# Products of zeros on TensorE ahead of ten steps of a two-block hybrid network

## The chip, the cores and the metric

One core of one Trainium2 chip runs the whole program in one launch. The metric is the device time of one execution in microseconds (us), as the median of several runs. TensorE is called PE in the profile, its weight loads PEld, VectorE DVE, ScalarE ACT, GpSimd POOL, and the queue that issues the DMAs SP.

## What is computed

256 tokens of width 1024 pass through two blocks of two layers each, all in float32.

```
# block 1, for each of 2 layers
h = x @ w_in                                  # q, k, v of three attentions, index, forget gate, gate
a  = subln(diff_attention(...)); b = sparse_attention(top 64); c = forgetting_attention(...)
mixed = concat(a, b, c) * silu(gate)
x = layer_norm(ALPHA * x + mixed @ w_out)
# block 2, for each of 2 layers; xs = 256 latent tokens, cs = 256 context tokens
hx = rms_norm(xs) * (1 + scale) + shift       # scale, shift, gate come from silu(c) @ w_mod
px = hx @ w_in + b_in
ya = conv_module(...)                         # depthwise convolution of 31 taps
yb = (rms_norm(gla_forward + gla_backward) * silu(gate)) @ w_gla_out     # gated linear attention
yc = (grouped_attention(...) * silu(gate)) @ w_attn_out
xs = xs + gate_x * ((sigmoid * ya + sigmoid * yb + sigmoid * yc) @ w_out)
```

## The kernel before

**How a product is made.** A float32 product is split. Each operand is written as hi + lo, both rounded to a float32 form that PE multiplies in one pass; three products (hi·hi, lo·hi, hi·lo) replace one. A weight piece of 128 x 1024 arrives by DMA (L3115), ACT makes its hi part (`cut_hi`, L1920) and DVE its lo part (`cut_lo`, L2340). Four cut pieces fit in block 1, three in block 2, so the cut of a piece waits until PE has finished with the one that had its place. Activations are turned by PE against the identity (`flip`, L1468), ACT takes the hi part from the bank (`flip_hi`, L1954), DVE the lo part (`flip_lo`, L2349). `project` is six products of 512 columns (L1541 to L1543; in block 2 a bias product, L1537, goes ahead), `project_t` the same for transposed outputs (L1559 to L1561).

**Order.** A planner writes one list of steps; each engine runs its own steps of that list strictly in order and waits on semaphores. An output bank of PE is taken in turn from a pool, and a step waits for the reader of its bank's last content (`before`).

**Places that the change touches.** `out1` is block 1's output projection: half 0 takes the mix in the order of parts 1, 0, 0, 2 (`MIX_PAIRS`), for two token tiles. The mix part 0 of a tile is ready late, at the end of the differential attention. After `out1` come the residual (L2563), the layer norm on DVE and POOL, and the flips of the new x (`flip x1`) for the next layer. `flip y1` turns the gated output of linear attention, which POOL makes (`gated`, L2995), after the token tiles' head norms, in POOL's order. `mod` are the products of block 2's modulation (L1482), put between block 1's steps. `in2` with chunk 3 (`KKV`) is the first projection of block 2's latent tokens.

The head of `project` before the change, which decides what PE waits for:

```python
        xh, xl = operand(kind, l, kp, t)
        pe.wait_ge("cut_lo", n)
        if kp == 0:
            pe.wait_ge(*(before or ()))
```

Of the kernel before, what the change touches and what calls it, by code (L numbers as in the profile page):

```python
# [8 lines left out]
F32, F32R, BF16 = mybir.dt.float32, mybir.dt.float32r, mybir.dt.bfloat16  # L9
# [3 lines left out]
P = 128  # L13
# [12 lines left out]
WC = 512  # L26
# [46 lines left out]
VAL, GLU, CGATE, KKV, GV, LRQ, AQ, GG, AG, M0A, M0B, M1A, M1B, M2A, M2B = range(len(CHUNKS2))  # L73
# [45 lines left out]
def tiles_of(layer):  # L119
    return EVERY if layer < LAYERS - 1 else X_TILES  # L120
# [22 lines left out]
def pipeline(items, stages, lags):  # L143
    for tick in range(len(items) + lags[-1]):
        for stage, lag in reversed(list(zip(stages, lags))):
            if 0 <= tick - lag < len(items):
                yield from stage(items[tick - lag])


def flip(source, l, t, g):  # L150
# [75 lines left out]
def attend(l, name):  # L226
    for qt in range(NT):
        key = lambda j: (l, name, qt, j)
        scores = lambda j: iter([[("att_s",) + key(j)]])
        top = lambda j: iter([[("att_max",) + key(j), ("att_exp",) + key(j), ("att_norm",) + key(j)]])  # L230
        turn = lambda j: iter([[("att_flip",) + key(j), ("att_t_act" if j % 2 == 0 else "att_t_dve",) + key(j)]])
        values = lambda j: iter([[("att_v",) + key(j)]])
        yield from pipeline(range(MAPS[name]), [scores, top, turn, values], [0, 1, 3, 4])
        yield [("att_out_diff", l, qt) if name == "diff" else ("att_out", l, name, qt)]
# [971 lines left out]
class Program:  # L1206
# [19 lines left out]
    def allocate(self, ctx):  # L1226
        nc = self.nc

        def sb(name, shape, dtype=F32, scope=ctx, side="left"):
            return scope.enter_context(nc.sbuf_tensor(name, shape, dtype, side=side))  # L1230

        m = self.m = Memory()
        m.ident, m.ones = sb("ident", [P, P]), sb("ones", [P, P])
        m.half = sb("minus_half", [P, 32])
        m.mod_cols = sb("mod_cols", [P, LAYERS * MOD_COLS])
        m.x = sb("x", [P, NT, D])
        m.raw = [sb(f"w_raw{i}", [P, KP * WC]) for i in range(RAW2)]
        m.hi = [sb(f"w_hi{i}", [P, KP * WC], F32R) for i in range(CUT2)]
        m.lo = [sb(f"w_lo{i}", [P, KP * WC], F32R) for i in range(CUT2)]
        b = self.b = Memory()  # L1240
        b.par, b.rows = sb("par2", [P, LAYERS, PAR_COLS]), sb("rows2", [P, LAYERS, 2 * P])
        b.bias, b.sel = sb("bias_parts", [96, LAYERS, WC], BF16), sb("bias_sel", [96, N_BIAS, P], BF16)
        b.ams, b.scale = sb("att_ms", [P, 2, 4, 3, 8]), sb("scale", [P, LAYERS, KD, 2])
        b.mod = m.mod_cols[:, :].rearrange("p (l a k s) -> p l a k s", l=LAYERS, a=3, k=KD)
        b.cos, b.sin = sb("cos2", [P, NT, HD]), sb("sin2", [P, NT, HD])
        b.tri2, b.halves = sb("tri2", [P, 4, P]), sb("halves", [P, 2])
        b.gmask = sb("gla_mask", [P, 4, P], mybir.dt.uint32)
        b.mean_w, b.ss, b.gms = sb("mean_w", [P, P]), sb("sum_sq", [P, 8]), sb("gla_ms", [P, 4, 8])


        with ExitStack() as one:
            own = lambda name, shape, dtype=F32, scope=one: sb(name, shape, dtype, scope)
            self.first_rest(own)
            self.first_branches(own)
        with ExitStack() as two:
            self.second_rest(lambda name, shape, dtype=F32: sb(name, shape, dtype, two))
            self.second_begin(lambda name, shape, dtype=F32, scope=two: sb(name, shape, dtype, scope))
        with ExitStack() as three:
            self.second_again(lambda name, shape, dtype=F32: sb(name, shape, dtype, three))
# [124 lines left out]
    def slot(self, *token):  # L1384
        return self.plan.slot[token]
# [74 lines left out]
def tensor_engine(k):  # L1460
    nc, m, b, slot = k.nc, k.m, k.b, k.slot
    pe = Queue(k, nc.tensor, "pe_own")
    mm = nc.tensor.matmul
    sem = k.sem

    def flips(ps, blocks, width=P):
        for i, block in enumerate(blocks):
            ins = nc.tensor.transpose(ps[0:width, i * P:(i + 1) * P], block, m.ident[:, :])  # L1468
        return ins

    def mod(l, c, kp):
        n = k.plan.piece_of["mod", l, c, kp]
        raw = k.piece(n, WC)[0].rearrange("p (k n) -> p k n", k=KP)
        i, before = slot("proj", "mod", l, c)
        pe.wait_ge("silu_in", 1)
        pe.wait_ge(*k.plan.arrived[n])
        if kp == 0:
            pe.wait_ge(*(before or ()))
        for kk in range(KP):
            q = kp * KP + kk  # L1480
            for j in range(4):
                ins = mm(k.bank[i][32 * j:32 * (j + 1), 0:P], m.c_pad[:, q, :], raw[:, kk, j * P:(j + 1) * P],  # L1482
                         start=q == 0, stop=q == KD - 1, tile_position=(0, 32 * j))
        ins.then_inc(sem["mod"], 1)
# [8 lines left out]
    def flip(source, l, t, g):  # L1493
        i, before = slot("aux", "flip", source, l, t, g)
        first, count = {"x1": X_BLOCKS, "mix": MIX_BLOCKS}.get(source, Y_BLOCKS)[g]
        src = {"x1": m.x, "mix": m.mix, "y1": b.gv}[source]
        if source == "x1" and l == 0:
            pe.wait_ge("first_in", 32)
        elif source == "x1":
            pe.wait_ge("ln_dve" if g == 0 else "ln_pool", l - 1, t)  # L1500
        elif source == "mix":
            pe.wait_ge("gate_mul", l, g, t)
        else:
            pe.wait_ge("gated", l, GG, t)
        pe.wait_ge(*(before or ()))
        ins = flips(k.bank[i], [src[:, t, (first + j) * P:(first + j + 1) * P] for j in range(count)])
        ins.then_inc(sem["flip"], 1)

    def operand(kind, l, kp, t):
        if kind == "in1":  # L1510
            pe.wait_ge("flip_lo", "x1", l, t, kp // 2)
            return m.xh, m.xl
        if kind == "out1":
            pe.wait_ge("flip_lo", "mix", l, t, MIX_PART[MIX_PAIRS[kp]])
            return m.xh, m.xl
        if kind in ("in2", "in2c"):
            pe.wait_ge("mi_lo", l, t, 4 * (kp // 2))
            return b.xh, b.xl
        pe.wait_ge("m_lo", l, 2 * kp + 1)
        return b.xh, b.xl  # L1520

    def project(kind, l, c, kp, t):
        n = k.plan.piece_of[kind, l, c, kp]
        width = k.width(n)
        raw, hi, lo = (x.rearrange("p (k n) -> p k n", k=KP) for x in k.piece(n, width))
        name, with_bias = ("in2", True) if kind in ("in2", "in2c") else (kind, False)
        w = 32 if with_bias and c == LRQ and t not in tiles_of(l) else width
        i, before = slot("proj", name, l, c, t)
        out, col = k.bank[i][:, 0:w], slice(t * P, (t + 1) * P)
        xh, xl = operand(kind, l, kp, t)  # L1530
        pe.wait_ge("cut_lo", n)
        if kp == 0:
            pe.wait_ge(*(before or ()))
        if kp == 0 and with_bias:
            pe.wait_ge("bias_sel")
            pe.wait_ge("bias0" if l == 0 else "bias1")
            mm(out, b.sel[:, c - 3, :], b.bias[0:96, l, 0:w], start=True, stop=False)  # L1537
        last = kp == NP - 1
        for kk in range(KP):
            q = (MIX_PAIRS[kp] if kind == "out1" else kp) * KP + kk  # L1540
            mm(out, xh[:, q, col], hi[:, kk, 0:w], start=kp == 0 and kk == 0 and not with_bias, stop=False)  # L1541
            mm(out, xh[:, q, col], lo[:, kk, 0:w], start=False, stop=False)  # L1542
            ins = mm(out, xl[:, q, col], hi[:, kk, 0:w], start=False, stop=last and kk == KP - 1)  # L1543
        ins.then_inc(sem["project"], 1)
# [779 lines left out]
def vector_engine(k):  # L2324
    nc, m, b, slot, sem = k.nc, k.m, k.b, k.slot, k.sem
    dve = Queue(k, nc.vector, "dve_own")
    v = nc.vector

    v.memset(m.c_pad[:, :, :], 0.0).then_inc(sem["c_zero"], 1)
    v.memset(m.ones[:, :], 1.0)  # L2330
    v.memset(m.half[:, :], -0.5).then_inc(sem["half_in"], 1)
    dve.wait_ge("consts_in", CONSTS)
    dve.wait_ge("first_in", 32)
# [831 lines left out]
def program(nc, io):  # L3165
    with ExitStack() as ctx:
        k = Program(nc, ctx, io)
        tensor_engine(k)
        scalar_engine(k)
        vector_engine(k)  # L3170
        gpsimd_engine(k)
        sync_engine(k)
# [111 lines left out]
```

## Time and profile before

| | |
|---|---|
| median of 3 runs | 1349.01 us (1348.95 to 1355.51) |
| the profiled execution, its own time | 1349.29 us, of it span 1348.0 us |
| mean granted TensorE clock over the span | 0.970 |
| PE busy | 1268.7 us, 94% of the span, 7856 instructions |
| PEld, DVE, ACT, POOL busy | 76%, 67%, 44%, 21% |
| HBM read | 165.79 MB, 124 GB/s over the span |

PE is busy nearly all the time, so the profile is read by PE's idle time and by the clock that it was granted: 1.00 is 2.4 GHz, 0.50 is 1.2 GHz. A row of the timeline gives the start, the duration, and in brackets how long the engine had been idle before and what ended that. Durations of products overlap, so the cost of one in a stream is the distance from start to start.

### The profile page before, as it was taken

To read this page: it belongs to the slowest core of one execution; us is meant where nothing else is said; L and a number is where in the kernel's file an instruction comes from. 1 tells how busy PE (TensorE), PEld (TensorE's weight loads), DVE (VectorE), ACT (ScalarE), POOL (GpSimd) and SP (SyncE) were. 2 spreads that over 40 slices of the span, in tenths; PEclk is the share of its full clock that TensorE was granted. 3 is DMA by queue.
4 is the path that set the end of the run, shared out by engine and by line. 5 is a ranking of instruction groups with operands and counts; after the bars stand their busy time and mean duration, and the time that the engine had idled before them with its cause. 6 is when DMAs were issued, how large, how long until landed. Compare 5 with 4: busy or idle time off the path is not lost. (4 is left out here: it accounts for less than half of the span.)

```text
span 1348.0 us, 19775 instructions
## 1 busy us (share of the span) xinstructions
PE 1268.7 (94%) x7856; PEld 1030.3 (76%) x7856; DVE 897.9 (67%) x1564; ACT 588.9 (44%) x986; POOL 288.0 (21%) x227
## 2 busy tenths in 40 slices
PE   7999987989988899999799999999999998889998
PEld 5777766867767677877577778888898877668997
DVE  4696665684576744379999854233786688876555
ACT  3444532434444564323234353243573555436443
POOL 0110012210021431235400012111452132100323
PEclk9999987989988999999899999999999998989999
DMA  7574465264342431112211222223552332204453
GB/s 255 210 279 152 157 224 182 94 244 170 124 166 75 138 120 54 63 48 78 63 63 63 63 63 85 102 94 95 195 179 96 98 115 89 79 32 143 139 182 116
DMA packets 49133, 168.12 MB, mean 125 GB/s; under 512 B 5841, under 2 KB 7057, under 8 KB 48785
## 3 DMA queue, kind: packets, MB, share of 16 engines
q1 hardware_dynamic: 49041, 166.86, 36.9%
q8 instruction: 62, 1.02, 0.3%
q14 instruction: 30, 0.25, 0.1%
HBM read 165.79 MB, written 1.05 MB: 124 GB/s over the span
## 5 line engine op out<-in xcount | busy, mean ns | idle before, releaser
L2340 DVE TENSOR_TENSOR w_lo<-w_raw,w_hi 128x1024 fp32r<-128x1024 f32 (+3 forms) x264 | 325.8, 1237 | 202.6 <-ACT w_hi L1920 201.8
L1920 ACT ACTIVATE w_hi<-w_raw 128x1024 fp32r<-128x1024 f32 (+3 forms) x264 | 269.9, 1027 | 395.6 <-PE bank L1543 122.8
L1541 PE MATMUL bank<-w_hi,x_hi 128*128 128x512 f32 (+4 forms) x736 | 300.1, 408 | 15.7 <-DVE x_lo L2349 9.1
L1543 PE MATMUL bank<-w_hi,x_lo 128*128 128x512 f32 (+4 forms) x736 | 282.0, 383 | 0.0
L1542 PE MATMUL bank<-w_lo,x_hi 128*128 128x512 f32 (+4 forms) x736 | 281.9, 383 | 0.0
L1559 PE MATMUL bank<-x_hi,w_hi 128*128 128x512 f32 (+1 forms) x640 | 225.8, 353 | 3.5 <-ACT conv_u L2137 2.1
L1561 PE MATMUL bank<-x_lo,w_hi 128*128 128x512 f32 (+1 forms) x640 | 217.1, 339 | 0.0
L1560 PE MATMUL bank<-x_hi,w_lo 128*128 128x512 f32 (+1 forms) x640 | 217.0, 339 | 0.0
L1541 PEld LDWEIGHTS bank<-w_hi,x_hi 128*128 128x128 f32 x736 | 142.2, 193 | 50.0 <-DVE x_lo L2349 11.7
L1543 PEld LDWEIGHTS bank<-w_hi,x_lo 128*128 128x128 f32 x736 | 141.5, 192 | 27.2
L1542 PEld LDWEIGHTS bank<-w_lo,x_hi 128*128 128x128 f32 x736 | 142.2, 193 | 22.1
L2660 DVE SCALAR_TENSOR_TENSOR conv_val<-conv_u,par,conv_val 128x512 f32<-128x512 f32 (+1 forms) x240 | 146.7, 659 | 0.0
L1559 PEld LDWEIGHTS bank<-x_hi,w_hi 128*128 128x128 f32 x640 | 122.9, 192 | 26.4 <-issue 13.0
L1561 PEld LDWEIGHTS bank<-x_lo,w_hi 128*128 128x128 f32 x640 | 122.7, 192 | 13.2
L1560 PEld LDWEIGHTS bank<-x_hi,w_lo 128*128 128x128 f32 x640 | 123.0, 192 | 11.8 <-issue 0.5
L2990 POOL TENSOR_TENSOR merged<-merged,sigma 128x512 f32<-128x512 f32 (+1 forms) x32 | 43.1, 1378 | 141.9 <-DVE sigma L2701 141.9
L1583 PE MATMUL bank<-y_hi,w_hi 128*128 128x512 f32 x96 | 38.6, 402 | 0.0
L1585 PE MATMUL bank<-y_lo,w_hi 128*128 128x512 f32 x96 | 37.5, 390 | 0.0
L1584 PE MATMUL bank<-y_hi,w_lo 128*128 128x512 f32 x96 | 37.4, 390 | 0.0
L3002 POOL TENSOR_TENSOR att_q<-att_q,gla_k_state 128x512 f32<-128x512 f32 x4 | 5.0, 1290 | 147.3 <-DVE att_q L2865 147.3
L2150 ACT ACTIVATE sigma<-bank,par 128x512 f32<-128x512 f32 (+1 forms) x48 | 27.4, 575 | 13.4 <-PE bank L1561 13.2
L2285 ACT ACTIVATE att_p<-bank,att_stat 128x512 f32<-128x512 f32 (+1 forms) x37 | 21.8, 591 | 24.1 <-DVE att_stat L2838 24.1
(357 smaller groups left out, 1865.8 us busy)
## 6 DMA issues: line engine op xcount, KB each, us to landing
w_raw<-in_w SPq DMA_DIRECT2D x172, 512.0 KB, 3.6
w_raw<-in_wm SPq DMA_DIRECT2D x48, 512.0 KB, 5.2
w_raw<-in_wo SPq DMA_DIRECT2D x40, 512.0 KB, 3.7
w_raw<-in_wy_gla SPq DMA_DIRECT2D x8, 512.0 KB, 3.6
w_raw<-in_wy_att SPq DMA_DIRECT2D x8, 512.0 KB, 3.5
w_raw<-in_wy_conv SPq DMA_DIRECT2D x8, 512.0 KB, 3.5
w_raw<-in_w SPq DMA_DIRECT2D x8, 460.0 KB, 4.7
w_raw<-in_w SPq DMA_DIRECT2D x12, 288.0 KB, 2.8
```

The lines of the kernel that those rows point to most:

```text
L1541: mm(out, xh[:, q, col], hi[:, kk, 0:w], start=kp == 0 and kk == 0 and not with_bias, stop=False)
L1542: mm(out, xh[:, q, col], lo[:, kk, 0:w], start=False, stop=False)
L1543: ins = mm(out, xl[:, q, col], hi[:, kk, 0:w], start=False, stop=last and kk == KP - 1)
L1559: mm(out, hi[:, kk, cols], b.xh[:, q, 0:n_tok], start=q == 0, stop=False)
L1560: mm(out, lo[:, kk, cols], b.xh[:, q, 0:n_tok], start=False, stop=False)
L1561: ins = mm(out, hi[:, kk, cols], b.xl[:, q, 0:n_tok], start=False, stop=q == KD - 1)
L1583: mm(out, hi[:, kk, cols], yh[:, q, 0:n_tok], start=q == 0, stop=False)
L1585: ins = mm(out, hi[:, kk, cols], yl[:, q, 0:n_tok], start=False, stop=q == 3)
L1920: do(hi, raw, ACT.Copy).then_inc(sem["cut_hi"], 1)
L2340: v.tensor_tensor(lo, raw, hi.bitcast(F32), ALU.subtract).then_inc(sem["cut_lo"], 1)
L2660: ins = v.scalar_tensor_tensor(out, src, taps[:, j, n:n + 1], out, ALU.mult, ALU.add)
L2990: g.tensor_tensor(out, out, b.sigma[:, j, 0:len(tiles_of(l)) * P], ALU.add).then_inc(sem["acc_add"], 1)
```

## The change

A tile `zeros` of 128 x 512 in bf16 is added, filled by one DVE memset at the start. In front of ten steps of PE a number of products of zeros is issued, 85 in all: each loads 128 x 128 zeros and streams 512 columns of zeros into the bank that the step is going to use. Where the bank is already being accumulated (the `out1` steps with kp above 0) they add zero; elsewhere they write zeros that the step's own first product or transpose overwrites. In `flip` and `project` the wait for the bank moves ahead of the waits for the operands, and the zeros stand between the two.

```diff
+FILLING = {("flip", "x1", 1, 0, 0): 4, ("flip", "x1", 1, 1, 0): 9, ("flip", "y1", 0, 0, 0): 30,
+           ("project", "out1", 0, 0, 0, 1): 4, ("project", "out1", 0, 0, 3, 1): 4,
+           ("project", "out1", 1, 0, 0, 1): 5, ("project", "out1", 1, 0, 1, 0): 7, ("project", "out1", 1, 0, 1, 1): 5,
+           ("project", "out1", 1, 0, 3, 1): 7, ("project", "in2", 0, KKV, 0, 1): 10}
...
-        m.ident, m.ones = sb("ident", [P, P]), sb("ones", [P, P])
+        m.ident, m.ones, m.zeros = sb("ident", [P, P]), sb("ones", [P, P]), sb("zeros", [P, WC], BF16)
...
+    def fill(step, i, opened):
+
+        pe.wait_ge("masks_in", 1)
+        for n in range(FILLING.get(step, 0)):
+            mm(k.bank[i][:, :], m.zeros[:, 0:P], m.zeros[:, :], start=not opened, stop=not opened)
...
         src = {"x1": m.x, "mix": m.mix, "y1": b.gv}[source]
+        pe.wait_ge(*(before or ()))
+        if ("flip", source, l, t, g) in FILLING:
+            fill(("flip", source, l, t, g), i, False)
         if source == "x1" and l == 0:
...
-        pe.wait_ge(*(before or ()))
         ins = flips(k.bank[i], [src[:, t, (first + j) * P:(first + j + 1) * P] for j in range(count)])
...
         out, col = k.bank[i][:, 0:w], slice(t * P, (t + 1) * P)
+        if kp == 0:
+            pe.wait_ge(*(before or ()))
+        if ("project", kind, l, c, kp, t) in FILLING:
+            fill(("project", kind, l, c, kp, t), i, kp > 0)
         xh, xl = operand(kind, l, kp, t)
         pe.wait_ge("cut_lo", n)
-        if kp == 0:
-            pe.wait_ge(*(before or ()))
...
     v.memset(m.ones[:, :], 1.0)
+    v.memset(m.zeros[:, :], 0.0)
```

A key reads (stage, source or kind, layer, ...): a flip's key ends in token tile and group, a projection's in chunk or half, kp and token tile. `in2` of layer 0 belongs to block 2.

## Rows read from the trace of the kernel before

**Rows 1.** The page's second part, TensorE's granted clock in 40 slices, in tenths.

```profile
PEclk9999987989988999999899999999999998989999
```

**Rows 2.** Busy time by stretch: PE, PEld, DVE, ACT, POOL, granted clock, DMA share, GB/s.

```profile
185.90:192.80 6.90, 6.36 (x18) 4.91 (x18) 3.40 (x7) 1.33 (x2) 0.00 (x0) 0.51 0.52 203
216.70:230.30 13.60, 9.67 (x43) 7.12 (x44) 8.82 (x12) 2.84 (x6) 7.24 (x5) 0.50 0.72 266
...
397.60:411.20 13.60, 9.99 (x29) 7.34 (x29) 5.02 (x9) 5.07 (x8) 1.10 (x2) 0.50 0.33 117
643.30:653.60 10.30, 5.30 (x15) 4.34 (x16) 7.94 (x11) 0.60 (x1) 10.19 (x7) 0.50 0.21 58
1117.80:1124.60 6.80, 4.57 (x16) 3.83 (x17) 6.80 (x12) 3.08 (x5) 0.82 (x1) 0.50 0.33 102
```

**Rows 3.** Timeline of PE, 228 to 232 us: the same products at either clock.

```profile
228.28 0.63 PE L1542 MATMUL bank<-w_lo,x_hi 128*128 128x512 f32 x1
228.70 0.63 PE L1543 MATMUL bank<-w_hi,x_lo 128*128 128x512 f32 x1
...
231.29 0.39 PE L1542 MATMUL bank<-w_lo,x_hi 128*128 128x512 f32 x1
231.52 0.39 PE L1543 MATMUL bank<-w_hi,x_lo 128*128 128x512 f32 x1
```

**Rows 4.** Timeline of DVE, ACT and PE, block 1 layer 1, 395 to 408 us.

```profile
395.45 0.68 DVE L2551 SCALAR_TENSOR_TENSOR gate<-gate,bank 128x512 f32<-128x512 f32 x1
...
396.85 0.50 PE L1541 MATMUL bank<-w_hi,x_hi 128*128 128x512 f32 x1 [1.29 <-DVE x_lo L2349]
...
399.28 1.06 ACT L1920 ACTIVATE w_hi<-w_raw 128x1024 fp32r<-128x1024 f32 x1 [5.51 <-PE bank L1543]
...
402.25 0.79 PE L1541 MATMUL bank<-w_hi,x_hi 128*128 128x512 f32 x1 [2.20 <-DVE x_lo L2349]
...
407.44 0.80 PE L1541 MATMUL bank<-w_hi,x_hi 128*128 128x512 f32 x1 [1.41 <-DVE x_lo L2349]
```

**Rows 5.** Timeline of DVE at the start.

```profile
7.88 0.23 DVE L2334 CAST causal_bias_bf<-causal_bias 128x128 bf16<-128x128 f32 x1 [6.57 <-DMA lam_consts<-in_lam_consts]
```

**Rows 6.** Timeline, block 1 layer 0, around `out1 0 0 0 1`: PE and ACT.

```profile
173.12 0.48 PE L1541 MATMUL bank<-w_hi,x_hi 128*128 128x512 f32 x1
...
177.15 0.28 ACT L1927 ACTIVATE mod_row<-bank 128x128 f32<-128x128 f32 x1 [1.32 <-PE bank L1482]
...
178.48 0.63 PE L1468 MATMUL bank<-ident,mix 128*128 128x128 f32 x4 [0.61 <-ACT prob_b L2013]
```

**Rows 7.** Timeline of PE, block 1 layer 0, at `out1 0 0 3 1`.

```profile
199.04 0.50 PE L1541 MATMUL bank<-w_hi,x_hi 128*128 128x512 f32 x1 [1.04 <-DVE x_lo L2349]
```

**Rows 8.** Timeline of PE, 218 to 227 us, between the two layers of block 1.

```profile
218.19 0.60 PE L1491 MATMUL bank<-ident,mod_row 128*128 128x8 f32 x2 [0.40 <-ACT mod_row L1927]
219.65 2.24 PE L1468 MATMUL bank<-ident,x 128*128 128x128 f32 x8 [0.87 <-DVE x L2583]
224.53 2.24 PE L1468 MATMUL bank<-ident,x 128*128 128x128 f32 x8 [2.64 <-DVE x L2583]
226.42 0.78 PE L1541 MATMUL bank<-w_hi,x_hi 128*128 128x512 f32 x1
```

**Rows 9.** Timeline of PE and DVE around `flip y1 0 0 0`, 648 to 660 us.

```profile
648.29 1.12 PE L1468 MATMUL bank<-ident,gla_v 128*128 128x128 f32 x4 [9.18 <-POOL gla_v L2995]
...
654.48 0.66 PE L1468 MATMUL bank<-ident,gla_v 128*128 128x128 f32 x4 [0.33 <-POOL gla_v L2995]
...
658.28 0.68 DVE L2349 TENSOR_TENSOR y_lo<-bank,y_hi 128x512 fp32r<-128x512 f32 x1
...
659.01 0.66 PE L1468 MATMUL bank<-ident,att_q 128*128 128x128 f32 x4 [1.62 <-DVE y_lo L2349]
```

**Rows 10.** Timeline of PE at `out1 1 0 3 1` and at `in2 0 3 0 1`.

```profile
419.25 0.50 PE L1541 MATMUL bank<-w_hi,x_hi 128*128 128x512 f32 x1 [2.06 <-DVE x_lo L2349]
...
460.49 0.39 PE L1537 MATMUL bank<-bias_parts,bias_sel 96*128 96x512 bf16 x1 [3.12 <-DVE x_lo L2647]
```

## The prediction

> **What bounds the kernel now.** I read the granted clock first, then PE's busy time by stretch, then PE's timeline around each of the ten steps. PE sets the pace for most of the span: it is busy 94% of it. So time is lost where PE stands still and where it runs at half clock. The clock line shows dips in some ten slices [rows 1]; cut to their edges they are stretches at 1.2 GHz, of which four lie near the edited steps: 6.9 us from 185.9, 13.6 from 216.7, 13.6 from 397.6 and 10.3 from 643.3 [rows 2]. PE is busy there for 6.4, 9.7, 10.0 and 5.3 us. A product of 512 columns costs 0.43 us from start to start at 1.2 GHz and 0.23 at 2.4 [rows 3], so what PE does in such a stretch takes nearly twice its time. Each of them begins shortly after PE had idled in pieces: ahead of 397.6 the piece is 1.29 us [rows 4]. The reader should see two things there. A longer clock is worth nothing by itself: it pays only where the next wait of PE ends with work that PE itself released. And zeros that outlast the wait they stand in delay everything behind them.
>
> **Price of a zero product.** The trace has no bf16 product of 512 columns followed by another one. The nearest row is the float32r product of the same width: 0.23 us at full, 0.43 at half clock [rows 3]; I take these. The lower bound is nothing, where it fits into a wait. The Trainium skill ("TensorE: Matmul & The Clock Gate", Part 1) gives 215.7 and 426.7 ns for a bf16 product of this width; by it the 85 products would take 1.2 us less at full clock, nearly all inside waits. The weight loads of zeros run beside the products, and the one memset on DVE falls into DVE's 6.57 us of waiting for the first DMAs [rows 5]: nothing.
>
> **Part by part.**
>
> `out1 0 0 0 1`, 4 zeros. At 173.12 PE had no idle time before it [rows 6], so 4 x 0.23 = 0.92 us is paid. The modulation products, ACT's copy of their row at 177.15 and the exponentials behind it all move, so the 0.61 us of idle at 178.48, which ACT ended, doesn't absorb it [rows 6]. I take 0.6 us, since DVE's own queue of cuts holds part of what follows anyway. Nothing here lifts the fall at 185.9. But that stretch starts and ends at instants that I see no reason to move, and work that comes 0.6 us later into a half-clock stretch loses only half: **+0.3 us** at 192.8 (0 to +0.9).
>
> `out1 0 0 3 1`, 4 zeros: 0.92 us in an idle time of 1.04 [rows 7], at full clock: **0**.
>
> `flip x1 1 0 0` and `1 1 0`, 4 and 9 zeros. The clock has already fallen at 216.7, after waits for DMAs that nobody fills [rows 2]. PE is free at 218.8 (0.60 after 218.19), so 4 x 0.43 = 1.7 us of zeros end at 220.5 to 220.8, not at 219.65, when DVE had delivered x [rows 8]. The eight transposes take 2.24 us and end near 222.9. Nine zeros at 0.43 are 3.9 us and end at 226.8, 2.3 us after the 224.53 at which the next transposes began. Against that stands the clock: before, it rose at 230.3, and from 226.42 only (230.3 - 226.42)/0.43 = 9 products were done. With PE at work from 218.8 without a pause, the rise comes earlier. If only at 226.9, the first projection starts at 227.9 and has (230.3 - 227.9)/0.23 = 10.4 products done: a gain of 1.4 x 0.23 = 0.3 us. If at 223.5, the nine zeros end at 225.2, the transposes are held by POOL and DVE as before, the projection starts at 226.3 and has up to 17.4 products done: a gain of 1.9 us. If never because of the zeros, it is a loss of 2.3 us. I take **-0.8 us**, the +0.3 from above included, because these counts are at the instant 230.3.
> The Trainium skill (the same page, Part 4) says that transposes don't count as work for the clock; then the 0.3 us end of this is the right one and the sum is 0.5 us smaller. The stretch agrees as far as it goes: 16 transposes stand in it and the clock stayed at 0.50, but idle time stands there too.
>
> `out1 1 0 0 1`, `1 0 1 0`, `1 0 1 1`, with 5, 7 and 5 zeros: here is the gain. The first of them waits for its bank, which DVE's L2551 releases at 395.45 + 0.68 = 396.13, inside the idle time; 5 x 0.23 = 1.15 us end at 397.28, so the step starts 0.43 us late [rows 4]. But PE no longer idles in pieces, and the clock should stay at 2.4 GHz through 397.6 to 411.2. Then the half of this step that ran slow takes 3 x 0.2 = 0.6 us less. The flip behind it gains nothing: ACT's cut at 399.28, released by the projection's end, is ahead of its hi part. The second projection takes 6 x 0.2 = 1.2 us less, its flip 1.12 - 0.66 = 0.46 us less [rows 9], the third projection 1.2, and the transposes up to 411.2 about 0.4. The seven zeros (1.6 us) and the five (1.15) fit into 2.20 and 1.41 us, and both waits end with hi and lo parts of what PE has just turned, so they move with PE. Sum: +0.43 - 0.6 - 1.2 - 0.46 - 1.2 - 0.4 = **-3.4 us** (-4.0 to +2.0). What follows to the end of block 1 is a chain of PE, residual and layer norm, so the gain is carried on.
>
> `out1 1 0 3 1` and `in2 0 3 0 1`: 7 zeros (1.6 us) in 2.06 and 10 (2.3 us) in 3.12 us of idle time [rows 10], at full clock before: **0**.
>
> `flip y1 0 0 0`, 30 zeros: 30 x 0.23 = 6.9 us in 9.18 us of idle time that POOL ends. The clock would no longer fall at 643.3, and the flip and the two `project_t` behind it, 6.2 us to 654.48, would take about 2.4 us less. But PE then meets two walls it doesn't set: the next flip at 654.48 waits for POOL's product, and the one at 659.01 for DVE's lo part of 658.28, in the order of DVE's taps [rows 9]. The gain becomes idle time: **0** (-2.4 to +0.3).
>
> The sum is -0.8 - 3.4 = -4.2 us. From the profiled execution's own 1349.3 us (1.3 us more than its span) that gives **1345.1 us**. The median of the runs is 1349.0, 0.3 us below that execution, which is within what I can resolve.
>
> **Rivals.**
> (1) The gain is lost to later falls of the clock. Some stretches at half clock lie behind the edits and are filled by nobody, such as 1117.8 [rows 2]. Their edges need not move with the kernel, so a kernel that arrives 4 us earlier may run more in them. One such stretch costs 1.5 to 3.4 us at half speed; one or two more give 1347.5 to 1350.
> (2) More is won. The clock rises at 223.5 (-1.1 us more) and the freed time at 654 reaches POOL or DVE after all (-2.4): 1345.1 - 3.5 = 1341.6, with the range 1339 to 1343. Against it: both releasers at 654 and 659 are other engines.
> (3) It ends slower: products of zeros don't hold the clock. Then they only cost: 0.9 at 173, 2.3 at 224, and in layer 1 0.43 + (7 x 0.43 - 2.20) + (5 x 0.43 - 1.41) = 2.0 us; the 30 run 18 at full and 12 at half clock, 9.3 us, in 9.18. Sum +5.2: 1354.5. It decides from the point where the clock still falls at 397.6. For it speaks only that no trace here shows zeros on PE.
> (4) The change does not do what it says in most places, since short waits don't matter. The Trainium skill (the same page, "Why this matters for your kernels") names a single long idle time as what drops the clock; by it only the 30 zeros could help. The kernel would then keep its fall at 397.6 and come out as in (3). The trace speaks against it: the clock fell there after no idle time above 1.29 us [rows 4].
>
> **How the numbers follow.** The forecast, 1343 to 1347.5, gets 0.50; rival 1 0.20; rival 2 0.22; rivals 3 and 4 together 0.08. The predicted time is 1345.1. The range holds the forecast, rival 1 and part of rival 2: 1340.0 to 1350.0. A measurement of this kernel tells about 0.5% from no change, which is 6.7 us: faster than 1342.3 or slower than 1355.8. Faster takes most of rival 2 and a little of the forecast's edge: 0.21. Slower takes half of rivals 3 and 4: 0.04. The rest, 0.75, is within 0.5%.
>
> **What would show each step.** The step at 173 starts 0.9 us later. The clock stands at 1.00 from 397 to 411, and the distance from the first projection of mix part 0 to the end of those flips is some 3.4 us shorter. In the stretch from 218 to 230 the clock rises earlier than at 230.3. Around 640 to 654 the clock stays up while the flip of the second token tile still waits for POOL, with some 2.5 us of idle time ahead of it. The prediction is wrong if the clock still falls at 397, if the zeros outlast their waits, or if the stretches behind 1100 change by more than the edits gave.

## The result and the profile after

The kernel after takes 1341.09 us (median of 7 runs, 1340.53 to 1346.71), the kernel before 1355.51 us in the 7 runs beside it (1348.95 to 1357.71). The ratio is 0.993 with a 95% interval of 0.990 to 0.996, so it is faster by 0.4 to 1.0%. Two later groups of runs gave 0.993 (0.991 to 0.995) and 0.994 (0.992 to 0.996) for the same kernel. The forecast was 1345.1 us, a gain of 4.2 on an execution of 1349.3. Measured in means, the gain is 11.3 us in these seven runs beside seven, and 8.6 and 8.0 us in the two later groups. One execution of the experiment `sixty` below took 1711.3 us at a mean granted clock of 0.688 and is left out of its mean and ratio.

One thing has to be said about the kernel before. The three runs shown ahead of the prediction hid how widely it scatters: in 31 runs of one group it took 1343.8 to 1350.0 us eighteen times and 1354.8 to 1356.9 us thirteen times, with nothing between. Its mean there was 1350.9 us, 1.6 above the execution that I had profiled, and the means of the two groups were 1347.4 and 1355.6. I call them the lower and the upper group. In the comparison above, four of the seven executions of the kernel before belong to the upper group. So I compare means below where a kernel scatters.

The stretches of the profile after that answer to [rows 2] (columns as there; the first two lie elsewhere than before):

```profile
149.40:152.90 3.50, 3.50 (x18) 3.50 (x18) 3.39 (x8) 1.91 (x5) 0.00 (x0) 0.51 0.41 142
190.40:193.80 3.40, 3.40 (x11) 2.61 (x10) 0.90 (x1) 1.33 (x2) 0.00 (x0) 0.50 0.66 214
217.70:224.50 6.80, 5.85 (x33) 3.72 (x34) 5.01 (x8) 1.65 (x4) 4.87 (x5) 0.50 0.95 340
397.60:411.20 13.60, 12.16 (x65) 8.77 (x64) 8.16 (x15) 8.36 (x17) 1.44 (x3) 1.00 0.39 128
417.00:424.00 7.00, 7.00 (x32) 5.72 (x31) 3.99 (x6) 1.06 (x1) 0.00 (x0) 1.00 0.30 102
640.00:651.00 11.00, 6.27 (x30) 3.64 (x27) 8.66 (x11) 0.60 (x1) 10.89 (x7) 1.00 0.17 54
651.20:654.60 3.40, 2.81 (x9) 2.45 (x10) 3.40 (x4) 0.60 (x1) 3.40 (x3) 0.50 0.29 118
1115.40:1122.20 6.80, 5.03 (x19) 4.27 (x20) 6.80 (x13) 3.53 (x6) 0.36 (x1) 0.50 0.45 132
```

The clock stands at 1.00 where it had been 0.50 for 13.6 us, at 397.6 to 411.2. Between the layers the half-clock stretch is 6.8 us long instead of 13.6, at 186 to 193 it is 3.4 instead of 6.9, and at 643 it has gone, but 3.4 us of it come back at 651.2. All stretches at half clock together shrink from 81.6 to 54.0 us (in such sums the last stretch counts to its own end, some 1.5 us behind the last instruction). The first line is new: the clock fell in the midst of dense work, ahead of every edit, and cost this execution some 1.5 us. That execution took 1346.7 us, the longest of the seven.

PE's timeline between the layers, which answers to [rows 8]. L1481 are the zeros. Line numbers have moved in this kernel: `flip`'s L1468 is L1474, `project`'s L1541 is L1557, and DVE's L2349 is L2366:

```profile
219.74 0.60 PE L1503 MATMUL bank<-ident,mod_row 128*128 128x8 f32 x2 [0.40 <-ACT mod_row L1943]
220.19 1.87 PE L1481 MATMUL bank<-zeros 128*128 128x512 bf16 x4
221.85 1.91 PE L1474 MATMUL bank<-ident,x 128*128 128x128 f32 x8
223.56 2.59 PE L1481 MATMUL bank<-zeros 128*128 128x512 bf16 x9
226.10 0.66 PE L1474 MATMUL bank<-ident,x 128*128 128x128 f32 x4
227.32 0.63 PE L1474 MATMUL bank<-ident,x 128*128 128x128 f32 x4 [0.56 <-DVE x_lo L2366]
227.70 0.48 PE L1557 MATMUL bank<-w_hi,x_hi 128*128 128x512 f32 x1
```

And at the late mix parts of layer 1, which answers to [rows 4]:

```profile
395.71 1.24 PE L1481 MATMUL bank<-zeros 128*128 128x512 bf16 x5
397.16 0.51 PE L1557 MATMUL bank<-w_hi,x_hi 128*128 128x512 f32 x1 [0.21 <-DVE x_lo L2366]
...
399.11 1.67 PE L1481 MATMUL bank<-zeros 128*128 128x512 bf16 x7
401.89 0.50 PE L1557 MATMUL bank<-w_hi,x_hi 128*128 128x512 f32 x1 [1.11 <-DVE x_lo L2366]
...
403.82 1.24 PE L1481 MATMUL bank<-zeros 128*128 128x512 bf16 x5
405.39 0.50 PE L1557 MATMUL bank<-w_hi,x_hi 128*128 128x512 f32 x1 [0.33 <-DVE x_lo L2366]
...
413.22 1.69 PE L1481 MATMUL bank<-zeros 128*128 128x512 bf16 x7
416.41 0.50 PE L1557 MATMUL bank<-w_hi,x_hi 128*128 128x512 f32 x1 [1.51 <-DVE x_lo L2366]
```

The zeros fit into every wait here, and each wait still ends with DVE's lo part, not with the zeros.

Around the gated output, which answers to [rows 9]:

```profile
636.20 6.65 PE L1481 MATMUL bank<-zeros 128*128 128x512 bf16 x30
645.55 0.65 PE L1474 MATMUL bank<-ident,gla_v 128*128 128x128 f32 x4 [2.70 <-POOL gla_v L3012]
...
651.79 1.08 PE L1474 MATMUL bank<-ident,gla_v 128*128 128x128 f32 x4 [2.82 <-POOL gla_v L3012]
...
656.22 0.66 PE L1474 MATMUL bank<-ident,att_q 128*128 128x128 f32 x4 [0.23 <-DVE y_lo L2366]
```

Against [rows 9] the idle time ahead of the second flip has grown from 0.33 to 2.82 us, by the 2.5 us that the faster clock gave to the work before it. From flip to flip it is 6.24 us, before 6.19.

### The profile page after: what moved, and what is told of

It reads as the page before. It is cut to its first block and busy times, and to the rows that moved or that the text cites. A ratio compares the mean times of both kernels' runs of the same rounds, so it can differ in the third digit from the quotient of the medians.

```text
span 1345.4 us, 19943 instructions
## 1 busy us (share of the span) xinstructions
PE 1280.8 (95%) x7941; PEld 1033.9 (77%) x7941; DVE 899.0 (67%) x1565; ACT 588.7 (44%) x986; POOL 285.0 (21%) x227
## 5 line engine op out<-in xcount | busy, mean ns | idle before, releaser
L1557 PE MATMUL bank<-w_hi,x_hi 128*128 128x512 f32 (+4 forms) x736 | 298.7, 406 | 11.9 <-DVE w_lo L2357 6.6
L1557 PEld LDWEIGHTS bank<-w_hi,x_hi 128*128 128x128 f32 x736 | 142.0, 193 | 46.4 <-issue 11.4
```

## The experiments

Where two profiles are compared step by step, the same step of PE is looked up in both, and the difference of its start times is followed along the kernel. It jumps where one of them loses or gains time.

Theory: idle pieces of PE drop the clock; zeros in them hold it; what is then won stays only where PE's own chain goes on. How many places fall in one execution depends on where the instants at which the clock can change lie against the kernel. Rivals: the scatter has another cause; one or two places make the whole gain; zeros without a wait only cost.

**before_again**: the kernel before, unchanged.

> The kernel before, unchanged, profiled a second time and timed against itself: ratio 1.000. Its times fell into two groups, 1349 and 1355.5 to 1357.7 us, while the kernel after stayed between 1340.5 and 1346.7. My theory: the instants at which TensorE's clock can change lie differently against the kernel from one execution to the next, and the kernel before has places where the one position costs some 7 us more of half clock than the other. Then a second profile of a 1356 us execution shows the same waits and longer or more stretches at 1.2 GHz, 10 us or more beyond the 81.6 us of the first profile. The rival: the two groups differ by something else, DMA landings for instance; then the stretches at half clock add up to the same and idle time of TensorE differs. If this profile is of a 1349 us execution, it decides only if its stretches lie elsewhere than the first one's.

Mean of 10 runs 1350.8 us, ratio 1.001 (0.998 to 1.004). Its profiled execution took 1355.7 us. Five of its stretches at half clock, with the columns as above:

```profile
184.90:191.80 6.90, 6.74 (x21) 5.38 (x20) 3.41 (x7) 1.33 (x2) 0.00 (x0) 0.51 0.66 255
396.60:406.80 10.20, 7.11 (x19) 5.34 (x20) 3.91 (x8) 2.69 (x4) 0.55 (x1) 0.50 0.46 154
420.50:423.90 3.40, 3.40 (x10) 2.61 (x9) 2.90 (x5) 1.06 (x1) 0.00 (x0) 0.50 0.00 1
461.40:468.20 6.80, 5.82 (x14) 4.57 (x15) 3.23 (x5) 1.06 (x1) 2.79 (x3) 0.50 0.17 51
649.10:656.00 6.90, 2.98 (x9) 2.57 (x10) 5.71 (x9) 0.60 (x1) 6.79 (x5) 0.51 0.26 76
```

And PE's timeline ahead of the third and the fourth:

```profile
419.54 0.50 PE L1541 MATMUL bank<-w_hi,x_hi 128*128 128x512 f32 x1 [3.03 <-DVE x_lo L2349]
...
462.38 0.61 PE L1537 MATMUL bank<-bias_parts,bias_sel 96*128 96x512 bf16 x1 [3.11 <-DVE x_lo L2647]
463.21 0.63 PE L1542 MATMUL bank<-w_lo,x_hi 128*128 128x512 f32 x1
```

The stretch at 397 is shorter here (10.2 us, not 13.6), PE so reached the wait ahead of 419.54 earlier and idled 3.03 us in it, not 2.06, and the clock fell behind it and again behind the wait of 3.11 us. That second wait is no longer than the one of 3.12 us at which the first profile kept its clock [rows 10]. Compared step by step with the first profile, this execution is 0.3 us later at 419.5, 4.6 us later behind 468 and 6.4 us later at its end; 1.7 us come in the last layer, where one stretch at half clock is 10.2 us long (1123.6 to 1133.8) and not 6.8. So 4.3 of the 6.4 us are lost at the two places that the prediction costed at nothing. Another 1.6 us are lost at 366, where no edit stands and the stretch at half clock is 6.8 us long and not 3.4. The half-clock time is 95.8 us in all, against 81.6.

**late_mix**: only the three places at 397 to 407.

```diff
-FILLING = {... ten entries ...}
+FILLING = {("project", "out1", 1, 0, 0, 1): 5, ("project", "out1", 1, 0, 1, 0): 7, ("project", "out1", 1, 0, 1, 1): 5}
```

> Only the 5, 7 and 5 products of zeros ahead of block 1 layer 1's three projections of the late mix parts. The prediction's sum puts -3.4 us here, of the whole -4.2; so 1345.6 where the kernel before takes 1349.0, and the clock at 1.00 from 397 to 411. Rival: this place was only a part, and most of the measured gain comes from elsewhere; then the time is above 1346 in the better executions and the ratio to before is 0.998 or more. A second reading of the same theory: if the kernel before's slower executions lose their time at this place, the slower group vanishes here and the median ratio is 0.995 or lower.

Mean 1346.65 us (1344.0 to 1349.0), ratio 0.9975 (0.9952 to 0.9998). Against the mean of 1350.85 in the 31 runs beside it that is -4.2 us, close to the -3.4 of the sum. But it comes in another way than told: the lowest runs are no lower than the kernel before's (1344.0 against 1343.8), and against the mean of its lower group, 1347.4, the gain is only 0.8 us; what has gone is the group at 1355. In its profile, 396 to 415 is free of a fall, and one stands behind the unfilled wait that follows, which is 3.02 us long here:

```profile
396.00:415.00 19.00, 16.64 (x88) 11.73 (x87) 12.67 (x21) 11.25 (x23) 3.50 (x4) 1.00 0.32 111
417.60:421.00 3.40, 3.40 (x9) 2.65 (x9) 2.37 (x5) 0.89 (x1) 0.00 (x0) 0.50 0.18 71
```

**ends_only**: only the two places behind them.

```diff
+FILLING = {("project", "out1", 1, 0, 3, 1): 7, ("project", "in2", 0, KKV, 0, 1): 10}
```

> Only the 7 zeros ahead of layer 1's last half of the output projection (419.25 in the first profile) and the 10 ahead of block 2's first latent projection (460.49). The prediction gave both zero. In the second profile of the kernel before, an execution of 1355.7 us, the clock fell at exactly these two places, at 420.5 for 3.4 us and at 461.4 for 6.8 us, and 13 of 31 executions of the kernel before took 1354.8 to 1356.9 us. Theory: these two falls are what parts the slow group; with the two places filled no execution is above 1352, and the mean of the runs falls from 1350.5 by about 3. Rival: the slow group stays, four in ten executions at 1355, the mean unchanged, because the falls only mark an execution that lost its time elsewhere.

Mean 1349.8 us against 1351.6 of the 31 runs beside it, ratio 0.999 (0.996 to 1.002): not told from no change. "No execution above 1352" was wrong: five of ten took 1352.4 to 1353.7 us. But only one was above 1353.5, where the kernel before had 14 of 31, up to 1359.0. I read it as the group moved down by some 2 to 3 us, the part of these two places. That reading rests on ten runs and is not shown. The profiled execution, of 1347.3 us, has no fall at the two places, but in it the stretch at the late mix parts was 3.4 us long with no zeros there, and 2.3 us of the 3.1 that the zeros win were won by chance.

**between**: only the 4 and 9 zeros between the layers.

```diff
+FILLING = {("flip", "x1", 1, 0, 0): 4, ("flip", "x1", 1, 1, 0): 9}
```

> Only the 4 and 9 products of zeros between the two layers of block 1. In the profile of the kernel after the clock rose there at 224.5 and not at 230.3, and the projection's third step began 0.5 us earlier although it came 2.2 us late into this stretch, so this part is worth -2 us or more when nothing precedes it: 1347. The prediction's value was -0.8 to -1.1: 1348. Rival: the zeros run at half clock past the moment at which VectorE delivers x and cost as much as the earlier rise gives, ratio 1.000.

Mean 1349.85 us against 1350.85, ratio 0.998 (0.996 to 1.000, its upper end at 1.0004). A gain of 1.0 us, not told from none. At its own place the profiled execution of 1348.0 us does gain 2.1 us against the first profile. And it shows the two falls of before_again, which cost the same 4.3 us in it:

```profile
412.90:416.30 3.40, 3.40 (x10) 2.62 (x9) 2.86 (x5) 1.06 (x1) 0.00 (x0) 0.51 0.00 1
453.80:460.60 6.80, 5.71 (x14) 4.48 (x15) 3.26 (x5) 1.06 (x1) 2.79 (x3) 0.50 0.17 51
```

So these two falls do not by themselves make an execution of 1355 us: this one lost less elsewhere (1.5 us less at 315, where a stretch has gone). No run of this kernel was above 1352.3, though nothing is filled at the two places. What parts the two groups therefore stays open.

**gated_only**: only the 30 zeros.

```diff
+FILLING = {("flip", "y1", 0, 0, 0): 30}
```

> Only the 30 products of zeros ahead of linear attention's gated output in layer 0 of block 2. The theory: the clock stays at 1.00 from 640 to 654, the two projections behind the flip end 2.4 us earlier, and that becomes idle time ahead of the next flip, which waits for GpSimd; time 0.0 us, 1349.0. Rival: what is freed reaches VectorE or GpSimd and about 2.4 us of it are kept, 1346.6.

Mean 1353.0 us against 1350.85, ratio 1.002 (0.999 to 1.005): no gain. Seven of its ten runs were above 1354. Its profiled execution, of 1356.9 us, was 6.0 us later than the first profile already ahead of the zeros, with the falls at 421.7 and 462.6 too, and it lost nothing at them. From flip to flip it takes 6.27 us, as in the kernel after. Its steps from 100 to 330 us keep within 0.2 us of one distance to the kernel before's, though the wait for the bank has moved ahead in all its flips and projections: the moved wait alone costs nothing that shows.

**five_places**: the places from 396 to 460 together.

```diff
+FILLING = {("project", "out1", 1, 0, 0, 1): 5, ("project", "out1", 1, 0, 1, 0): 7, ("project", "out1", 1, 0, 1, 1): 5,
+           ("project", "out1", 1, 0, 3, 1): 7, ("project", "in2", 0, KKV, 0, 1): 10}
```

> The 5, 7, 5, 7 and 10 zeros from 396 to 460 us, that is the late mix parts and the two places after them, without those of layer 0 and without the 30. If the theory holds, these five are nearly the whole change: mean 1343 to 1345, against 1341.8 of the kernel after (7 runs) and 1350.5 of the kernel before. Rival: layer 0's four places carry as much; then the mean is 1346 to 1348, no better than the late mix parts alone (1346.7).

Mean 1346.2 us against 1351.6, ratio 0.9963 (0.9934 to 0.9992). The mean lies in the rival's range; as a difference, -5.4 us, it is between the two. By subtraction from the 8.6 us of after_again beside it, some 3 us of the whole change's gain are left for layer 0's places and the 30 zeros.

**without_173** and **without_173_b**: the kernel after without the 4 zeros that meet no idle time.

```diff
-           ("project", "out1", 0, 0, 0, 1): 4, ("project", "out1", 0, 0, 3, 1): 4,
+           ("project", "out1", 0, 0, 3, 1): 4,
```

> The kernel after without the 4 zeros at 173 us, which meet no idle time. In the profile of the kernel after they ran from 175.40 to 176.43 and the step behind them came 0.7 us later; of that about 0.3 should be left after the half-clock stretch that follows: mean 0.3 us better than the kernel after (prediction's value; 0 to 0.9). Rival: even there they help to hold the clock in some executions; then the mean is up to 1 us worse.

> Again without the 4 zeros at 173. Its first ten runs had a mean of 1344.9, against 1342.6 in 17 runs of the kernel after, the opposite of the 0.3 us gain that the prediction gives. In its profile the clock was at half speed from 184.0 to 190.8, in a second profile of the kernel after it did not fall there at all. New theory: zeros without idle time ahead of them still help, because they push TensorE's work towards the wait at 183 (8.6 us after the step in one profile, 8.2 in the other), which shortens that wait; the difference of 2 us stays. Rival: it was the luck of the executions; then the means are within 1 us, or this one is better.

The first ten runs have a mean of 1344.9 us, the six of the second group 1343.8. The kernel after beside them has 1343.0 (10 runs) and 1345.5 (7 runs). So once it is 1.9 us slower and once 1.7 us faster: the time doesn't decide, and what these four zeros are worth stays open within some 2 us. The clock does show something. In the nine profiles of kernels without them, the stretch near 186 is 6.8 to 6.9 us long every time. In the four with them and no other edit near it, it is 3.4 (kernel after), 0 (after_again), 3.4 (after_third) and 6.9 us (sixty). The profiles of without_173 and without_173_b also show a cost of the 30 zeros that the kernel after's three do not. The wait ahead of the second flip, grown to 2.81 us, is followed by a fall that the kernel before doesn't have at this place:

```profile
645.64 1.08 PE L1474 MATMUL bank<-ident,gla_v 128*128 128x128 f32 x4 [2.81 <-POOL gla_v L3012]
```

The clock was at 0.50 for 6.8 us from 644.8, the next wait of PE is gone, and the steps behind it come 1.0 us later, measured against the steps ahead of the zeros. more_places shows the same, with 1.1 us.

**after_again** and **after_third**: the kernel after, unchanged.

> The kernel after, unchanged, profiled and timed once more beside the others. The first profile, an execution of 1346.7 us, had a stretch at half clock from 149.4 to 152.9 that no profile of the kernel before shows and in which 1.2 to 1.9 us were lost. Theory: its usual executions of 1340.5 to 1341.8 us don't have it, and otherwise look like the first profile from 218 to 660 us. Mean of the runs 1341 to 1343, ratio to before 0.993 to 0.995.

> The kernel after once more, as the measure for the other three of this group: mean 1342.6 of its 17 runs so far, between 1340.5 and 1346.9.

Means 1343.0 us (1340.9 to 1346.9) and 1345.5 (1344.2 to 1346.9), ratios 0.993 and 0.994. The two groups ran on different chips. Beside after_again, the kernel before had 14 of 31 executions in its upper group and a mean of 1347.9 in the lower one. So some 4.9 of the 8.6 us are a gain on the lower group, and the other 3.7 are that no execution is in an upper one. after_again's profiled execution took 1341.0 us:

```profile
184.00:194.00 10.00, 8.49 (x82) 6.86 (x83) 5.12 (x9) 1.76 (x3) 0.00 (x0) 1.00 0.73 276
215.20:218.70 3.50, 3.40 (x13) 1.81 (x11) 2.10 (x4) 0.77 (x2) 3.03 (x3) 0.51 1.02 405
393.00:425.00 32.00, 29.05 (x141) 21.53 (x139) 21.85 (x31) 16.09 (x27) 3.50 (x4) 1.00 0.33 109
447.00:470.00 23.00, 21.60 (x116) 17.54 (x117) 14.58 (x23) 11.43 (x18) 8.34 (x9) 1.00 0.52 155
629.00:655.00 26.00, 18.60 (x97) 12.51 (x98) 23.62 (x28) 5.43 (x9) 18.98 (x11) 1.00 0.20 65
```

No fall near 186, at 393 to 425, at 447 to 470 or at 629 to 655; between the layers 3.5 us are left; 40.6 us at half clock in all. Stepwise against the first profile of the kernel before, it is 0.7 us ahead at 150, 2.9 at 196 (a gain of 2.2, what the zeros cost already taken off), 5.0 behind the layers' boundary (2.1 more), 8.2 at 419 (3.1 more) and 8.3 at its end. So this execution has neither the fall at 149, as expected, nor the one at 651, which I had expected to stay; the fall at 149 came again in after_third's profiled execution of 1346.9 us.

**sixty**: the kernel after with 60 zeros ahead of the gated output.

```diff
-           ("flip", "y1", 0, 0, 0): 30,
+           ("flip", "y1", 0, 0, 0): 60,
```

> The kernel after with 60 instead of 30 zeros ahead of the gated output. 30 took 6.65 us in its profiles, so 60 take 13.3 us, where TensorE is free 9.2 us ahead of the flip: the flip comes 4.1 us late. Theory: of this 2.8 us were slack ahead of the next flip, which waits for GpSimd, so the kernel loses 1.3 to 4.1 us: mean 1344 to 1347. Rival: the slack hides it all, mean as of the kernel after.

```profile
631.74 13.12 PE L1481 MATMUL bank<-zeros 128*128 128x512 bf16 x60
644.70 0.60 PE L1474 MATMUL bank<-ident,gla_v 128*128 128x128 f32 x4
...
647.90 0.60 PE L1474 MATMUL bank<-ident,gla_v 128*128 128x128 f32 x4
...
651.83 0.66 PE L1474 MATMUL bank<-ident,att_q 128*128 128x128 f32 x4 [1.06 <-DVE y_lo L2366]
```

1341.7 to 1342.6 us in three runs, no slower than the kernel after beside them: the rival was right. Against after_third's profile, from which this execution differs by 4.5 us ahead of the zeros, the first flip comes 3.6 us late, the second 0.6 and the flip behind DVE's lo part 0.1. The two walls of the prediction, POOL and DVE, take up an overrun of 3.6 us as they take up a gain of 2.5.

**more_places**: the kernel after with nine further places.

```diff
+           ("flip", "mix", 0, 1, 0): 3, ("project", "out1", 0, 0, 1, 1): 2, ("aq_flip", 1, 0): 10, ("aq_flip", 1, 2): 5,
+           ("a_flip", 1, 0, 3): 7, ("a_s", 1, 0, 3): 6, ("a_flip", 1, 0, 5): 3, ("a_s", 1, 1, 1): 5, ("project_t", 1, M0A, 0, 0): 8}
```

The new steps take the wait for their bank ahead of the zeros and the waits for their operands behind them, as the others do.

> The kernel after with nine further places filled, where its profiles still show idle pieces ahead of a fall of the clock: 3 and 2 zeros at 183 to 187 us (block 1 layer 0, late mix part of the second tile), and in the last layer 10 and 5 ahead of two flips of the queries (idle 2.8 and 1.4 to 1.8 us), 7, 6, 3 and 5 in the attention (idle 1.95, 1.7, 0.9, 1.4), 8 ahead of the first merge projection of the convolution branch (idle 2.1). In the profiles of the kernel after the clock stood at half speed there for 3.4 to 7, 7, 3.4 and 3.4 us. Theory: where what follows is TensorE's own chain, half of each is won: 1 to 3 us on the mean of the runs, 1340 to 1342. Rival: the attention's chain there belongs to VectorE and ScalarE, as after the 30 zeros, and the zeros that wait for a bank or outlast their wait cost as much: mean as of the kernel after, 1342.6, or up to 2 us worse.

Mean 1344.5 us (6 runs) against 1345.5 of the kernel after beside it, 0.9933 against 0.9943: not told apart. The half-clock time fell to 35.9 us, the least of all, and the time did not follow. In the last layer, one place even lost what had been won:

```profile
1241.26 3.21 PE L1483 MATMUL bank<-zeros 128*128 128x512 bf16 x8 [2.04 <-ACT conv_u L2163]
1243.91 0.77 PE L1579 MATMUL bank<-x_hi,w_hi 128*128 128x256 f32 x1
```

The bank came free only when ACT had emptied it, after 2.04 us, which is about when the operands were ready too. So nothing of the wait was filled, the clock fell all the same (1241.7), the zeros ran at half clock, and the step was 2.6 us later against the kernel after's profile than the steps ahead of it. 1.7 us of that are still there at the end.

**The places across all fourteen profiles.** At the late mix parts the clock fell in all five profiles without zeros there, for 3.4 to 13.6 us, and in none of the nine with them. Between the layers the stretch is 13.6 to 13.7 us long in all six profiles without zeros there and 3.4 to 6.8 in the eight with them. At the two places behind the late mix parts, the clock fell at the first in four of five profiles without zeros and at the second in three, for 1.6 and 2.7 us of time, and in none of the nine with them. At the first of the two, PE's wait was 3.02 or 3.03 us in the four with a fall and 2.06 in the one without. At the second it was 3.1 to 3.2 us in all five. So its length doesn't decide there, and the theory's free instants remain as the explanation that fits; no run moves them on purpose.

## Why the prediction was right in kind and too small

The time of 1341.1 us lies in the stated range, but the outcome that the prediction held likeliest, within 0.5% of no change, did not come; faster had 0.21. The place of the main gain and its mechanism were as told. The sum was too small, and that the forecast of 1345.1 is only 4 us off is in part luck of its base: it was worked out from an execution of the lower group. Against the lower group alone the gain of 4.9 us in after_again's runs is near the 4.2 forecast; the 3.7 us that come from having no upper group are what the sum has no term for.

- **Price of a zero.** 30 zeros took 6.65 us, 0.22 each, and 4 at half clock 1.87, 0.47 each with the last one's tail counted in. The 0.23 and 0.43 taken from the float32r rows were good.
- **`out1 0 0 0 1`.** The step's first product came 0.7 us late and its second 0.8, not 0.92. "Nothing here lifts the fall at 185.9" was wrong in the traces: it was shorter in three of four profiles. The instants that the prediction took as fixed are not: without zeros there the stretch began at 184.0 to 186.8. A cause that would fit is that the zeros push PE's work towards the idle pieces: ahead of the flip of the second tile's late mix part (183.33 in the first profile) the kernel before has 1.16 us idle, after_again 0.88. That was argued from the profiles and not shown by a time.
- **Between the layers.** The clock rose at 224.5, the second of the three cases, and PE went into the projection at full speed. The profile after gains 2.1 us here, as do after_again, sixty and the profile of the kernel with this part alone, whose mean gained 1.0. So the -0.8, which has the loss of 0.3 at 186 in it, was too small by 1.0 us here; the 1.9 us of the second case was nearly right. The 0.3 us end, which the prediction tied to transposes not counting as work for the clock, did not come, though eight of them (1.91 us) stand in the stretch before the rise.
- **Late mix parts.** The mechanism was as told: clock at 1.00, each wait ended by DVE, ACT's cut ahead of the first hi part. Two terms were off. The bank was free: the gate product that PE's zeros wait for is the one of token tile 0, some 5 us earlier, not that at 395.45, so the zeros began at 395.71 right behind the attention's values and the +0.43 did not arise. And of 4.1 us won by the last transpose of the late mix parts 1.0 was lost in the next wait, ahead of 416.41 (1.69 us of zeros and 1.51 idle, before 2.06), since DVE, ACT and POOL were then busy with the context's norm. Left were 3.15 us, against 3.4. That is against the first profile, where this stretch was the longest of the five without zeros; in ends_only's 2.3 us of it were there without any zeros.
- **The two places behind.** This is the step that failed: "at full clock before: 0". It was true of one profiled execution, which is the exception: of the five profiles without zeros there, three show both falls, for 10.2 us in all and 4.3 us of time, and a fourth the first. Thirteen of 31 executions of the kernel before are as long as the second profile of it, but whether they have these falls is not shown. The five places from 396 to 460 together gave 5.4 us in the mean, 2 more than the 3.4 of the sum for the first three. The rest that the sum lacked lies, by the profiles, in layer 0, at 186 and between the layers, where the sum took a gain of 0.8 us in all (a loss of 0.3 at 186 included) for what were gains of 2.2 and 2.1 in after_again.
- **Gated output.** Right in the kernel after's three profiles: the clock was up, the 2.5 us gained became idle time ahead of the next flip, and gated_only and sixty show no change either way. But that idle time can drop the clock itself: in without_173, without_173_b and more_places it cost 1.0 to 1.1 us, more than the +0.3 at the end of this term's range.
- **Rival 1**, later falls that eat the gain, is in no profile of the kernel after but in others: the first stretch of the last layer was 10.2 us long instead of 6.8 in six of the fourteen profiles, without_173 and without_173_b among them, which lost 2.8 us there against the first profile. How often the kernel after meets it, three profiles don't tell. Up to 1260 us the last layer's stretches at half clock sum to 20.5 us in the first profile of the kernel before, to 20.4 in the profile after and to 17.2 in after_again. Rivals 3 and 4 are excluded by the clock of 1.00 at 397.6 to 411.2 in the kernel after and by the nine profiles with zeros there of which none fell, against five of five without.

The rule of the Trainium skill ("TensorE: Matmul & The Clock Gate", "Why this matters for your kernels") that one long idle time drops the clock doesn't cover this kernel: filling idle pieces of 1.3, 2.2 and 1.4 us kept it at full speed, and filling the long one of 9.18 us was worth nothing in time.

## What to carry to other kernels

Where PE's clock falls behind scattered waits, fill the waits whose releaser hangs on PE itself; a wait that another engine's chain ends gives nothing back, however much half clock it removes, and the idle time that it moves to the next wait can drop the clock there (1.0 us lost in three profiles). Profile such a kernel more than once before costing an edit at nothing: a wait that kept its clock in one execution may lose it in the next. Zeros belong behind a bank that is free early, since they cost nothing only inside a wait that they can enter at its start.

## What the runs showed of the hardware that I had not expected

The same program falls into two groups of executions (1343.8 to 1350.0 and 1354.8 to 1356.9 us, with nothing in the 4.8 us between) on a single core, with 81.6 and 95.8 us at half clock in one profile of each. The clock can also fall in dense work without any idle time: from 149.4 to 152.9 PE was busy for all 3.5 us, at 0.51, in two of the fourteen profiles of this study (the profile after and after_third's), while after_again's, of the same kernel, has no fall there. Ahead of it PE had been busy for 9.29 of 9.4 us at 1.00. And less half clock is not less time: 54.0, 40.6 and 35.9 us of it went with 1346.7, 1341.0 and 1345.6 us. A wait of 3.1 to 3.2 us kept the clock in two executions and lost it in three.
